# A dense feed-forward without its closing products of zeros, its residual additions made in the next layer's block

## The reference, cut to what matters

```python
for l in range(DEPTH_2):                                  # 2 layers
    h = rmsnorm(x, ln1_g[l]) * (1.0 + sc1) + sh1
    z = h @ w_in[l]
    ...                                                   # recurrence and attention
    x = x + g1 * (jnp.concatenate([lru, att], axis=-1) @ w_out[l])
    h = rmsnorm(x, ln2_g[l]) * (1.0 + sc2) + sh2
    if l % 2 == 0:
        f = swiglu(h, ffn_w_gate[j], ffn_w_up[j], ffn_w_down[j])
    else:
        f = moe(h, moe_router[j], moe_w_gate[j], moe_w_up[j], moe_w_down[j])
    x = x + g2 * f
return rmsnorm(x, final_g)
```

## Time and profile before

| | us |
|---|---|
| median of 3 runs | 2777.84 |
| lowest and highest of them | 2774.09, 2779.42 |
| span of the profiled execution | 2777.3 |
| TensorE busy in it | 2625.4 (95%) |
| VectorE busy | 1987.1 (72%) |
| ScalarE busy | 1387.2 (50%) |
| mean granted clock of TensorE | 0.966 |

### The profile page before, as it was taken

The page is one execution under the profiler, slowest core; times in us unless marked ns, Lnnn a source line. Parts: engine busy times, 40 slices in busy tenths (PEclk is TensorE's granted clock), DMA queues, the critical chain, the costliest instruction groups (busy, mean ns, idle before and its releaser), DMA issues. The chain is left out here.

```text
span 2777.3 us, 42352 instructions
## 1 busy us (share of the span) xinstructions
PE 2625.4 (95%) x14630; PEld 2265.1 (82%) x14630; DVE 1987.1 (72%) x2713; ACT 1387.2 (50%) x1699; POOL 0.2 (0%) x4
## 2 busy tenths in 40 slices
PE   8979878999999999999798998988999999999998
PEld 3769768888788889999687998876888888888886
DVE  6768235988777877776553653527898898898896
ACT  3444224133444444444343443326777777777775
POOL 0000000000000000000000000000000000000000
PEclk8989899999999999999899999998999999999999
DMA  6531223632678877877251554516999999999995
GB/s 243 212 114 46 69 76 123 185 119 77 226 262 295 299 277 246 291 245 248 75 189 55 183 181 141 175 51 237 357 365 339 354 362 340 356 361 339 371 343 201
DMA packets 223291, 626.83 MB, mean 226 GB/s; under 512 B 15297, under 2 KB 23521, under 8 KB 222817
## 3 DMA queue, kind: packets, MB, share of 16 engines
q1 hardware_dynamic: 223200, 625.64, 63.8%
HBM read 619.29 MB, written 6.29 MB: 225 GB/s over the span
## 5 line engine op out<-in xcount | busy, mean ns | idle before, releaser
L3157 DVE TENSOR_TENSOR wide_low<-wide,wide_high 128x2048 fp32r<-128x2048 f32 x288 | 656.8, 2289 | 97.9 <-ACT wide_high L3100 95.3
L3100 ACT ACTIVATE wide_high<-wide 128x2048 fp32r<-128x2048 f32 x288 | 552.4, 1918 | 179.4 <-PE bank L2990 141.9
L229 DVE TENSOR_TENSOR expert_tile_low<-slot,expert_tile_high 128x1024 fp32r<-128x1024 f32 x216 | 263.8, 1223 | 132.4 <-ACT expert_tile_high L221 128.2
L221 ACT ACTIVATE expert_tile_high<-slot 128x1024 fp32r<-128x1024 f32 x216 | 227.4, 1054 | 191.4 <-PE bank L238 83.6
L2986 PE MATMUL bank<-wide_high,xg_high 128*128 128x512 f32 x768 | 304.1, 396 | 4.3 <-ACT wide_high L3100 4.3
L2987 PE MATMUL bank<-wide_high,xg_low 128*128 128x512 f32 x768 | 300.3, 391 | 0.0
L2990 PE MATMUL bank<-wide_low,xg_high 128*128 128x512 f32 x768 | 206.1, 390 | 0.0
L237 PE MATMUL bank<-h_high,expert_tile_high 128*128 128x256 f32 x704 | 173.6, 284 | 0.0
L238 PE MATMUL bank<-h_low,expert_tile_high 128*128 128x256 f32 x704 | 173.0, 283 | 0.0
L1899 PE MATMUL bank<-expert_tile_high,act_hi 128*128 128x512 f32 x512 | 161.2, 396 | 12.2 <-DVE act_lo L2040 12.2
L2986 PEld LDWEIGHTS bank<-wide_high,xg_high 128*128 128x128 f32 x768 | 144.8, 189 | 33.4 <-ACT wide_high L3100 4.5
(11 more groups left out here) (508 smaller groups left out, 5125.6 us busy)
## 6 DMA issues: line engine op xcount, KB each, us to landing
wide<-in_moe_gu SPq DMA_DIRECT2D x192, 1024.0 KB, 5.4
wide<-in_moe_d SPq DMA_DIRECT2D x96, 1024.0 KB, 5.6
slot<-in_peer_u SPq DMA_DIRECT2D x128, 512.0 KB, 4.3
slot<-in_peer_v SPq DMA_DIRECT2D x128, 512.0 KB, 4.4
slot<-in_w_in SPq DMA_DIRECT2D x72, 512.0 KB, 3.5
picked_or_ada<-in_ada_w SPq DMA_DIRECT2D x48, 512.0 KB, 4.9
ada_slot<-in_ada_w SPq DMA_DIRECT2D x48, 512.0 KB, 4.5
slot<-in_ffn_gu SPq DMA_DIRECT2D x48, 512.0 KB, 3.3
```

Of the source, the lines that this page charges most:

```text
L221: core.nc.scalar.activation(self.tile_hi[:, place % 2], core.slot[u][:], ACT.Copy).then_inc(self.hi_ready.sem, 1)
L229: core.nc.vector.tensor_tensor(self.tile_lo[:, place % 2], slot[:], self.tile_hi[:, place % 2].bitcast(F32), ALU.subtract)\
L3100: nc.scalar.activation(w_hi[n % NB][:].rearrange("p c n -> p (c n)"), wide[n % U][:], ACT.Copy).then_inc(hi_ready.sem, 1)
L3157: nc.vector.tensor_tensor(w_lo[n % NB][:].rearrange("p c n -> p (c n)"), wide[n % U][:], w_hi[n % NB][:].rearrange("p c n -> p (c n)").bit ...
```

## The change

The four products of zeros that close the feed-forward's banks are left out, with the semaphore they raised. `feed_forward` no longer adds to x. In layer 1's `mix_layer`, VectorE first waits until all tiles of the feed-forward are used and then makes the same eight additions from the same banks, with a semaphore count for each. ScalarE's squares in `first` wait chunk by chunk for that count, as they do in `second`. The bank in which `first` sums its squares is 0 instead of 5 in layer 1, since bank 5 now still holds chunks 2 and 3. Layer 0's `mix_layer` is as before.

```diff
-                mix_layer(core, c1, a, l, x, m, cos, sin, hide, lam, None if moe else lambda u: a["ffn_gu"][u % 2, u // 2])
+                mix_layer(core, c1, a, l, x, m, cos, sin, hide, lam, None if moe else lambda u: a["ffn_gu"][u % 2, u // 2], core.mod2[:, 40:48, 0] if moe else None)
...
-                    feed_forward(core, c1, a["ffn_gu"], a["ffn_d"], lambda u: a["w_in_2"][20 + u], x, m(5))
+                    feed_forward(core, c1, a["ffn_gu"], a["ffn_d"], lambda u: a["w_in_2"][20 + u])
...
-def mix_layer(core, ctx, a, l, x, mods, cos, sin, hide, lam, next_tiles):
+def mix_layer(core, ctx, a, l, x, mods, cos, sin, hide, lam, next_tiles, before_gate):
...
-    first = NormParts(core, ctx, f"before_{l}", x, h, core.gain[:, l, 0], mods(0), core.bank[5])
+    first = NormParts(core, ctx, f"before_{l}", x, h, core.gain[:, l, 0], mods(0), core.bank[5 if before_gate is None else 0])
+    ffn_added = core.count("ffn_added")
...
-            first.squares(act)
+            first.squares(act, None if before_gate is None else lambda c: act.wait_ge(ffn_added.sem, ffn_added.at(c + 1)))
...
+            if before_gate is not None:
+                dve.wait_ge(used.sem, used.at(0))
+                for t in range(C):
+                    nc.vector.scalar_tensor_tensor(x[:, t, :], out_at(t), before_gate[:, t:t + 1], x[:, t, :], ALU.mult, ALU.add)\
+                        .then_inc(ffn_added.sem, 1)
             first.vector(dve)
...
-            for b in range(4, 8):
-                last = nc.tensor.matmul(core.bank[b][:, :].rearrange("p (o n) -> p o n", o=4), core.zeros[:], core.zeros[:].rearrange("p (o n) -> p o n", o=1).broadcast_to([P, 4, P]), start=False, stop=True, skip_group_check=True)
-            last.then_inc(read.sem, 1)
...
-            dve.wait_ge(read.sem, read.at(1))
-            for m in range(C):
-                nc.vector.scalar_tensor_tensor(x[:, m, :], core.bank[4 + m // 2][:, (m % 2) * N:(m % 2) * N + N], gate[:, m:m + 1], x[:, m, :],
-                                               ALU.mult, ALU.add).then_inc(read.sem, 1)
```

More of the change, by code:

```diff
@@ L2647, in mix_layer @@
                      (flip_kept, 4), (o_made, 2), (o_squared, 8), (o_rooted, 1), (o_recip, 1), (o_normed, 2), (o_turned, 2), (heads_mixed, 2),
-                     (out_made, 4), (out_added, 8), (used, T)):
+                     (out_made, 4), (out_added, 8), (ffn_added, 0 if before_gate is None else C), (used, T)):
         count.passed(k)
@@ L2782, in route, with feed_forward @@
             c.passed(k)
-def feed_forward(core, ctx, gu, down, next_tiles, x, gate):
+def feed_forward(core, ctx, gu, down, next_tiles):
     nc = core.nc
@@ L2795, in feed_forward @@
     used, free = core.tiles_used, core.pair_free
-    silued, ready, read, own = core.count("ffn_silu"), core.count("ffn_hidden"), core.count("ffn_read"), core.count("ffn_vector_steps")
+    silued, ready, own = core.count("ffn_silu"), core.count("ffn_hidden"), core.count("ffn_vector_steps")
     R1, R2 = 2 * FT // U, FT // U
@@ L2892, in feed_forward @@
     own.passed(FT)
-    read.passed(1 + C)
     halver.passed(U * R, True)
```

## The result

The changed kernel took 2764.24 us (median of 5 runs, 2763.04 to 2774.80), the kernel before 2774.09 in the runs beside it (5 runs, 2772.45 to 2779.42): ratio 0.9963, 95% interval 0.9945 to 0.9981. Timed once more in a later session it stood at 2764.49 (6 runs) against 2774.97 (12 runs), ratio 0.9966 (0.9952 to 0.9979). It is faster, by some 10 us: a difference clear of the runs' spread, though only 0.4% of the time. The forecast was 2768.9 in a range from 2764.5 to 2773.0: the direction held, the time lies 0.3 us under the range.

The account below looks back on a forecast made before the run. At the seam before layer 1 only one engine works at a time, and everything waits for the root. Last product to root shrinks from 14.23 to 5.29 us, 8.94 less: 2777.84 - 8.9 = 2768.9 us, range 2764.5 to 2773.0.

Parts of the forecast that it names:

- Products of zeros, 3.44 us on the path: Feed-forward's end: leaving out the closing products of zeros saves 3.44 us, since VectorE waited for them.
- End of the block with TensorE last, taken as 0.30: Hand-over from TensorE's last feed-forward product to the first addition: between 0.03 and 0.50 us, taken as 0.30.
- Additions 3.23, squares done 0.46 behind: Layer 1's first norm: eight moved additions take 3.23 us; ScalarE's last square ends 0.46 us after them.
- Products of the squares at the full clock: TensorE in layer 1's first norm: full clock, one pair per 0.45 us, done at 1721.95 instead of 1731.70.
- The table load ends last, root at +5.29: ScalarE before layer 1's root: uncovered table load, 1.30 us, ends last; root 5.29 us after the last product, not 14.23.
- Tile 0 at half clock: Layer 1's first weight tile: still at half clock, 6.75 us; full clock would give 3.0 us more, 11.9 in all.
- The forecast is 2777.84 - 8.9: Whole kernel: median of three runs, 2777.84 us, less the seam's gain of 8.9, giving 2768.9.
- The clock under the squares: Rival in layer 1's first norm: TensorE's clock falls during the squares' products, gain only 6.2 us; chance 0.12 with non-overlap.
- additions and squares don't overlap: Rival in layer 1's first norm: squares end 2.4 us later, gain 6.5; chance 0.12 together with the clock's fall.
- The drain: Rival before layer 1's root: switching tables holds ScalarE longer, 1.28 us, gain 7.7; a drain would be a case; chance 0.04.
- Given back later: Rival behind the seam: one or two more half-clock stretches, about 3.0 us each, leave 5.9 or 2.9 gained; chance 0.11.
- The slower case: Rival in the routed layer's eight rounds: worse instruction fetching, 1.8 us per round, kernel at 2783.3 us; chance 0.03.

Follow-up runs that it names:

- the run with the tables early: Changed kernel plus a one-column root on ScalarE behind the dense feed-forward's last silu, loading the root's tables there; single run, root at +5.07, no time compared.
- the filler: Changed kernel plus four products of zeros behind the squares' products in layer 1's first norm: 2763.1 us, ratio 0.9966 to the kernel before.

## Why the prediction was right or wrong, point by point

- **Products of zeros, 3.44 us on the path.** Right: leaving them out alone took 3.5 to 3.7 from the last product to the root.
- **End of the block with TensorE last, taken as 0.30.** Right: 0.32 or 0.33 in every profile in which the additions are moved.
- **Additions 3.23, squares done 0.46 behind.** Right: 3.23 and 0.44.
- **Products of the squares at the full clock.** Right (3.72 us), and the run with the squares held back shows the other case: 6.52. My 0.45 a chunk behind the last square missed that they start only at +1.31 and are then limited by TensorE: done at +5.03, where I had +4.45.
- **The table load ends last, root at +5.29.** Right: +5.31. The load began 0.02 after the last square and ended at +5.30, and the root began 0.01 later, so no drain stands before or behind it. With the drain of about 1380 ns that the Trainium skill (ScalarE: Activation LUTs, What ACT_TABLE_LOAD costs) adds to every switch, the root would have come 1.38 later, an estimate from the page's figure; this trace does not show such a drain. The load ended 0.27 after the products of the squares, not 0.84, as the run with the tables early confirms (root 0.24 earlier). So TensorE's pause ahead of tile 0 grew from 3.50 to 3.75 us, not to 4.3.
- **Tile 0 at half clock, "I take the same".** This term was mis-sized: 6.75 us were assumed, 5.42 measured. It took 5.41 or 5.42 us in all five profiles where the squares overlap and no filler stands behind them, and 6.61 to 6.75 in the four where they don't overlap: 1.2 to 1.3 us more gain, where I had put up to 3.0 into the range. The clock now falls only after tile 0 has begun (1733.5, against 1732.16), where it had been at half from the first product. Nine profiles agree on this; but layer 0's tile 0, which ran in both forms with nothing changed, warns that such a term can go either way.
- **"The forecast is 2777.84 - 8.9".** This is the step that failed: its start, and the 1.4 us that the range allows for the runs' spread. The gain is 9.85 by the medians of the five runs each, and 10.25 in the traces (8.92 to the root, 1.33 in tile 0), close to the 8.94. But the start was a median of three. Beside the change, before's median was 2774.09, and 2776.76 over 35 runs whose ends lie 15.5 apart. Of the 4.66 us between 2768.9 and 2764.24, 3.75 are that shift and 0.91 the gain. The range gave the spread 1.4 us, where I had myself noted 5.33 among three runs. Part of this is chance. Before's medians in the four later sessions are 2776.76, 2774.97, 2775.07 and 2777.73, so the start was 0.1 to 2.9 too high against those, and 3.75 against the five runs beside the change; and 2776.76 less the traces' 10.25 is 2766.5, inside the range.
- **The profile's span and the median.** I set 2777.3 beside 2777.84 as nearly one. In four later profiles the profiled execution's own time is 1.8 us above its span (2766.24 for 2764.4, 2774.71 for 2772.9, 2760.05 for 2758.3, 2761.93 for 2760.1); taking the same here, it took about 2779.1 (an estimate); 12 of the 35 were longer.
- **Rivals.** The clock under the squares: refuted in the change. Its companion, that additions and squares don't overlap, was refuted too, but the prediction priced it at 2.4 us, for ScalarE alone; the run with the squares after all additions shows 5.30, since the clock falls with it. The drain: refuted. Given back later: not in the change (1035.42 against 1035.35), but in part with the filler. The slower case, the rounds of the routed layer: from its first product with expert weights (1896.98 before, 1892.61 after) to the start of VectorE's last low parts of its outputs (2756.20, 2751.85) it took 859.22 us before and 859.24 after; refuted.

## What to carry to other kernels

At a seam of one engine after another, read the relay from the last product to the next and add it up from rows of the same kernel; up to the root it came out within 0.1 us here. Overlapping two short steps is worth more than their length where it keeps TensorE's pause short enough that the clock stays up. A sum of 9 us in 2777 needs its start from many runs, or, better, is given as a difference: here three runs placed the start 3.75 us off, against an effect of 10. And a stretch behind a pause of TensorE has to be read in more than one profile: the same code ran 2.8 us longer or shorter by the clock alone.

## What the runs showed of the hardware that was not expected

- Products of zeros count as work for TensorE's clock: with four of them in a pause of 3.75 us, tile 0 took 3.72 us instead of 5.42, and 3.72 or 3.73 in all four kernels with such a filler.
- The same code after the same pause can run at either clock. Layer 0's tile 0, after 3.50 us of idleness, took 6.36 to 6.40 us in four profiles and 3.73 in six others without a filler; the products of the last norm's squares, after 2.60, took 5.14 to 5.41 in nine and 3.72 in one.
- Keeping the clock up in one pause can cost part of the gain in the next: 1.7 us gained in tile 0, about 1 given back at the routing, whose own code was the same and whose idle time nearly so (8.13 and 8.22 us). It was so in all three kernels with four products (27.05 to 27.11 us, against 26.03 to 26.26 in nine without).
- The clock can fall under work, when the idleness ahead of it is over: with 2.11 us of idleness ahead of them, the router's eight products began at the full clock at 1851.75, had it at half from 1853.0 to 1856.0, and took 5.31 us.
